# Mixers of the second block: sixteen 256-column fills in three rounded products, with the weight parts made by GpSimd

## The reference, cut to what matters

```python
x = x + 0.5 * swiglu_ffn(x, ffn1_norm[l], ffn1_wi[l], ffn1_wo[l])
h = rms_norm_2(x, mix_norm[l])
(sb_q, sb_k, sb_v, mla_cq, mla_ckv, mla_kr, nsa_q, ck, cv, sk, sv, wk, wv,
 nsa_gate, merge_gate) = jnp.split(h @ w_in[l], offsets, axis=-1)
# three attentions: o_sb, o_mla, o_nsa
y = sigmoid(merge_gate)[0] * (o_sb @ proj_sb[l]) + ...   # three branches
x = x + y @ w_out[l]
x = x + 0.5 * swiglu_ffn(x, ffn2_norm[l], ffn2_wi[l], ffn2_wo[l])
```

## Time and profile before

| | us |
|---|---|
| median of 3 runs (2702.73 to 2706.56) | 2703.87 |
| the profiled execution | 2706.46 |
| its span | 2705.2 |
| first mixer: features begin, attentions begin, output products begin | 1465.7, 1521, 1728.7 |
| second mixer: attentions begin, output products begin | 2235.5, 2444.4 |

### The profile page before, as it was taken

How to read it: one execution, slowest core, us unless ns; L and a number is a source line. 1 busy time by engine, 2 the same in 40 slices (tenths; PEclk the granted TensorE clock), 3 DMA queues, 4 the chain that set the end, 5 groups by cost and what they waited for, 6 DMA issues and landing times.

```text
span 2705.2 us, 28728 instructions
## 1 busy us (share of the span) xinstructions
PE 2298.7 (85%) x12062; PEld 1395.7 (52%) x12062; DVE 1087.7 (40%) x1748; ACT 805.9 (30%) x1178; POOL 1.2 (0%) x5
## 2 busy tenths in 40 slices
PE   7987666667877667666999999999999999999999
PEld 4632111113552111112888644678888885447887
DVE  2331000103651000103765543667667554446774
ACT  3321000002430000002444432544454344235543
POOL 0000000000000000000000000000000000000000
PEclk8999888888989888888999999999999999999999
DMA  9799999999649999999756432356566573225662
GB/s 380 300 369 421 421 422 421 421 422 371 247 156 414 421 421 421 421 421 360 200 189 169 163 108 91 124 146 191 191 174 187 187 197 115 94 78 151 173 191 78
DMA packets 329905, 705.23 MB, mean 261 GB/s; under 512 B 15889, under 2 KB 227089, under 8 KB 277552
## 3 DMA queue, kind: packets, MB, share of 16 engines
q1 hardware_dynamic: 329776, 703.40, 71.0%
HBM read 702.30 MB, written 1.05 MB: 260 GB/s over the span
## 4 chain that ended last, share of the span: by engine, by line
PE 63%; DMA 27%; DVE 5%; ACT 3%; issue 1%; SPq 1%; DVEq 0%; ACTq 0%
PE psum L870 60%; DMA ring<-in_moe_w_up 12%; DMA ring<-in_moe_w_down 6%; DMA ring<-in_moe_w_gate 5%; PE psum L874 3%; DVE arena L2232 1%; DMA arena<-in_moe_w_gate 1%; DMA arena<-in_moe_w_down 1%; DMA arena<-in_moe_w_up 1%; DMA ring<-in_ada_w 1%; ACT ring L1699 1%; DVE lent_r L2232 1%; SPq L712 1%; ACT xn L1699 1%; DVE ring L2232 1%
## 5 line engine op out<-in xcount | busy, mean ns | idle before, releaser
L870 PE MATMUL psum<-ring,arena 128*32 128x512 f32 (+2 forms) x3208 | 607.1, 666 | 243.8 <-DMA ring<-in_moe_w_up 86.0
L870 PE MATMUL psum<-lent_r 128*128 128x512 f32 (+1 forms) x3344 | 610.9, 345 | 3.0 <-DVE lent_r L2232 2.9
L870 PEld LDWEIGHTS psum<-lent_r 128*128 128x128 f32 x3344 | 524.6, 189 | 89.4 <-issue 6.9
L870 PEld LDWEIGHTS psum<-ring,arena 128*32 128x32 f32 (+2 forms) x3208 | 153.5, 128 | 670.1 <-issue 217.4
L2232 DVE TENSOR_TENSOR lent_r<-ring,lent_r 128x2048 fp32r<-128x2048 f32 (+1 forms) x158 | 347.0, 2197 | 206.2 <-ACT lent_r L1699 206.2
L1699 ACT ACTIVATE lent_r<-ring 128x2048 fp32r<-128x2048 f32 (+1 forms) x158 | 290.2, 1842 | 293.0 <-PE psum L870 216.6
L1699 ACT ACTIVATE arena<-psum 128x512 f32<-128x512 f32 (+2 forms) x103 | 55.5, 575 | 826.4 <-PE psum L870 781.3
L870 PE MATMUL psum<-ring,hT 128*128 128x512 f32 x512 | 243.0, 607 | 8.5 <-ACT ring L1699 5.5
L870 PE MATMUL psum<-lent_r,arena_r 128*128 128x512 f32 x1056 | 242.4, 391 | 0.0
L870 PE MATMUL psum<-arena 128*32 128x512 f32 (+6 forms) x648 | 196.4, 497 | 33.4 <-DMA arena<-in_moe_w_up 7.8
L2232 DVE TENSOR_TENSOR arena<-psum,arena 128x512 f32<-128x512 f32 (+2 forms) x21 | 20.3, 978 | 506.1 <-PE psum L870 506.1
(11 more groups left out here) (182 smaller groups left out, 1632.8 us busy)
## 6 DMA issues: line engine op xcount, KB each, us to landing
ring<-in_moe_w_up SPq DMA_DIRECT2D x120, 1024.0 KB, 26.7
ring<-in_moe_w_gate SPq DMA_DIRECT2D x119, 1024.0 KB, 26.7
ring<-in_moe_w_down SPq DMA_DIRECT2D x112, 1024.0 KB, 27.0
ring<-in_ffn_wi SPq DMA_DIRECT2D x176, 512.0 KB, 5.1
ring<-in_w_in SPq DMA_DIRECT2D x46, 1024.0 KB, 5.2
ring<-in_ffn_wo SPq DMA_DIRECT2D x44, 1024.0 KB, 4.9
ring<-in_ada_w SPq DMA_DIRECT2D x43, 1024.0 KB, 10.2
arena<-in_moe_w_gate SPq DMA_DIRECT2D x9, 1024.0 KB, 26.3
```

What stands on the lines that cost most here:

```text
L870: return T.matmul(out, lhsT, rhs, start=start, stop=stop, **kw)
```

## The change

Each mixer's fills become 16 fills of 256 columns (`FILLS`, `FILL_W`) for all 256 tokens: for each of the two token halves 8 x 3 rounded products into one half of bank 7. A fill again has four steps, of twelve products each, and one copy by ScalarE behind it. The rounded high part of a fill's weights is made by GpSimd's `tensor_copy` into one of two slots (`mx.fill_high`), and the low part by GpSimd's `tensor_tensor` in place of the landed weights.

The unsplit `hT` isn't written any more. `mx.hT_high` takes its place in memory, and `mx.hT_low` lies in ring slot 4. Slots 5 and 6 hold the high parts of the weights and slot 7 still NSA's rows. So the ring rotates over slots 0 to 3 in the second block; slots 5 to 7 join it for the loads of a mixer's features and tokens (`order[:0] = extra`) and leave it again behind them (`given_back`).

```diff
 def fill_loads(layer, i):
-    for h in range(2):
-        load(("fill", layer, i, h), E.fill.at(layer, i, 1, h), half_chunk(A["w_in_2"][layer], h, fill_cols[i], 512))
+    for n in (2 * i, 2 * i + 1):
+        load(("fill", layer, n), E.fill.at(layer, n), cols_chunk(A["w_in_2"][layer], fill_cols[n], FILL_W))
...
 def mixer(layer):                                     # SyncE
+    order[:0] = extra
...
+    lend(own[:split_at])
+    given_back.append([owner[n] for n in extra])
...
-        lend(own[:-2])
+        lend(own[:split_at])
...
 def fillers():                                        # TensorE
-    for n in range(8):
-        slots = [got["fill", l, n, s] for s in range(2)]
+    for n in range(FILLS):
+        w = (mx.fill_high[n % 2], rounded_slot(got["fill", l, n][0]))
+        if n:
+            T.wait_ge(*E.filled.at(l, n - 1))
+        T.wait_ge(*E.fill_low.at(l, n))
         for t in range(TT):
-            if n + t:
-                T.wait_ge(*(E.filled.at(l, n, 0) if t else E.filled.at(l, n - 1, 1)))
...
-                    i = mm(psum[:, 7, :], hT[:, s * 4 + k, t * P:(t + 1) * P], slot[:, k * 512:(k + 1) * 512],
-                           s + k == 0, s * 4 + k == KT - 1)
...
+            tok = slice(t * P, (t + 1) * P)
+            for k in range(KT):
+                i = mm3(psum[:, 7, t * FILL_W:(t + 1) * FILL_W], (high[:, k, tok], low[:, k, tok]),
+                        tuple(v[:, k * FILL_W:(k + 1) * FILL_W] for v in w), k == 0, k == KT - 1)
+                if k == 3 or (k == 7 and t == 0):
+                    yield
+        i.then_inc(*E.fill.inc(l, n))
...
-                if k == 0 and u in norm_of_mix:        # VectorE
-                    whole_hT(u, scale, (0,))
...
 def gpsimd_program():
...
+    for layer in range(2):
+        for n in range(FILLS):
+            slot, *landed = got["fill", layer, n]
+            G.wait_ge(*landed)
+            G.wait_ge(*(E.fill.at(layer, n - 2) if n >= 2 else given_back[layer][n]))
+            G.tensor_copy(mx.fill_high[n % 2], slot).then_inc(*pool.own())
+            G.wait_ge(*pool.now)
+            G.tensor_tensor(rounded_slot(slot), slot, mx.fill_high[n % 2].bitcast(F32), ALU.subtract).then_inc(
+                *E.fill_low.inc(layer, n))
```

More of the change, by code:

```diff
@@ L42 @@
 LENT = 6
+SPLIT = 4
+FILLS, FILL_W = 16, 256
 LAST_SLOT = 13024
@@ L317, in build @@
     lent_r = nc.alloc_sbuf_tensor_at("lent_r", [P, LENT * SLOT], F32R, offset=ring_at + (N_SLOT - LENT) * SLOT * 4)
+    hT_r = nc.alloc_sbuf_tensor_at("hT_r", [P, KT, S], F32R, offset=hT_at)
+    own_r = nc.alloc_sbuf_tensor_at("own_r", [P, N_SLOT - LENT, SLOT], F32R, offset=ring_at)
     busy_r = nc.alloc_sbuf_tensor_at("busy_r", [P, 512], F32R, offset=gates_at)
@@ L462, in build @@
     cut_bufs[("mi", 0)] = cut_bufs[("mi", 1)] = [(a.take(SLOT, rounded=True), a.take(SLOT, rounded=True)) for _ in range(2)]
-    mx.hT_high, mx.hT_low = a.take(KT, S, rounded=True), a.take(KT, S, rounded=True)
+    split_at = N_SLOT - LENT - SPLIT
+    mx.hT_high, mx.hT_low = hT_r, own_r[:, split_at, :].rearrange("p (k s) -> p k s", k=KT)
+    mx.fill_high = [own_r[:, split_at + 1 + n, :] for n in range(2)]
     a, r = arena_from(0), lent_from(0)
@@ L608, in build @@
     E.mi_dve = Event(nc, "mi_dve", keys(2, [("f", n) for n in range(0, 10, 2)] + [("t", n) for n in range(2)]))
-    E.fill = Event(nc, "fill", keys(2, 8, TT, 2))
-    E.filled = Event(nc, "filled", keys(2, 8, TT))
+    E.fill_low = Event(nc, "fill_low", keys(2, FILLS))
+    E.fill = Event(nc, "fill", keys(2, FILLS))
+    E.filled = Event(nc, "filled", keys(2, FILLS))
     E.busy = Event(nc, "busy_rows", keys(1))
@@ L641, in build @@
     slot_of = [ring_sb[:, n, :] for n in range(N_SLOT)] + [arena[:, LAST_SLOT:LAST_SLOT + SLOT]]
-    act, dve = Line(nc, "act"), Line(nc, "dve")
-    got = {}
+    act, dve, pool = Line(nc, "act"), Line(nc, "dve"), Line(nc, "pool")
+    got, given_back = {}, []
     E.stored = nc.alloc_semaphore("s_stored")
@@ L663, in parts, with rounded_slot @@
         return cut_bufs[st, c][(p + (st == "ff" and c % 2 == 0)) % 2]
+    def rounded_slot(slot):
+        return own_r[:, next(n for n in range(split_at) if slot_of[n] is slot), :]
     def turned_in(u, k):
@@ L695, in build @@
     at_turns = [8, 9, 10, 11, 0, 1, 2, 3, 4, 5, 6, 7]
-    fill_cols = [C_NQ, C_SK] + [C_MERGE + br * D + n * 512 for br in range(3) for n in range(2)]
+    fill_cols = [c0 + n * FILL_W for c0, width in ((C_NQ, 512), (C_SK, 512), (C_MERGE, 3 * D)) for n in range(width // FILL_W)]
     mi_features = [C_SBQ, C_SBQ + 256, C_SBK, C_SBK + 256, C_CK]
@@ L791, in mixer @@
             w = A["w_in_2"][layer]
+            order[:0] = extra
+            if layer:
+                owner[extra[0]], owner[extra[1]], owner[extra[2]] = E.fill.at(0, FILLS - 2), E.fill.at(0, FILLS - 1), E.ns_pe.at(0, KT - 1)
             for i, c0 in enumerate(mi_features):
@@ L961, in to_hT @@
                     turn(k, 1).then_inc(*E.hT_pe.inc(u, k))
-                T.wait_ge(*(E.hT_whole if u in norm_of_mix else E.hT_dve).at(u, 0))
+                T.wait_ge(*E.hT_dve.at(u, 0))
                 turn(KT - 1, 0)
@@ L1594, in fillers @@
             def fillers():
-                for n in range(8):
-                    slots = [got["fill", l, n, s] for s in range(2)]
-                    for t in range(TT):
-                        if n + t:
-                            T.wait_ge(*(E.filled.at(l, n, 0) if t else E.filled.at(l, n - 1, 1)))
[L1600 to L1603, removed]
-                                i = mm(psum[:, 7, :], hT[:, s * 4 + k, t * P:(t + 1) * P], slot[:, k * 512:(k + 1) * 512],
-                                       s + k == 0, s * 4 + k == KT - 1)
[L1606 to L1611, removed]
+                for n in range(FILLS):
[3 more added lines that the diff above has]
+                    T.wait_ge(*E.fill_low.at(l, n))
+                    for t in range(TT):
+                        tok = slice(t * P, (t + 1) * P)
[5 more added lines that the diff above has]
+                    i.then_inc(*E.fill.inc(l, n))
+                    filled[0] += 1
+                    yield
             def nsa_all():
@@ L1642, in mixer @@
                 if br == 1:
-                    T.wait_ge(*E.filled.at(l, 7, 1))
+                    T.wait_ge(*E.filled.at(l, FILLS - 1))
                 for h in range(2):
@@ L2149, in fillers @@
             def fillers():
[L2150 to L2159, removed]
+                for n in range(FILLS):
+                    yield
+                    yield
+                    yield
+                    C.wait_ge(*E.fill.at(l, n))
+                    out, c0 = ((mx.nq, 0), (mx.kv, 0), (mx.merge[:, 0], 0), (mx.merge[:, 0], 512), (mx.merge[:, 1], 0),
+                               (mx.merge[:, 1], 512), (mx.merge[:, 2], 0), (mx.merge[:, 2], 512))[n // 2]
+                    c0 += n % 2 * FILL_W
+                    af(out[:, :, c0:c0 + FILL_W], psum[:, 7, :].rearrange("p (t c) -> p t c", t=TT), ACT.Copy).then_inc(
+                        *act.ev(E.filled, l, n))
+                    filled[0] += 1
+                    yield
             def nsa_all():
@@ L2171, in nsa_squares @@
                     next(fill)
-                C.wait_ge(*E.filled.at(l, 1, 1))
+                C.wait_ge(*E.filled.at(l, 3))
                 af(xn[:, :, 0:512], mx.nq, ACT.Square)
@@ L2356, in scaled_hT @@
                     *dve.ev(E.hT_dve, u, k))
-                if k == 0 and u in norm_of_mix:
-                    whole_hT(u, scale, (0,))
-        def whole_hT(u, scale, ks):
-            for k in ks:
-                ts(hT[:, k, :], psum[:, turned_in(u, k), 0:S], scale[:, k:k + 1]).then_inc(*dve.ev(E.hT_whole, u, k))
         def add_gated(st, which, u, banks=(0, 1, 2, 3)):
@@ L2888, in over @@
                 return a.unsqueeze(1).unsqueeze(1).broadcast_to([P, 2, 2, n])
+            V.wait_ge(*given_back[l][2])
             for t in range(TT):
@@ L2966, in mixer @@
             scaled_hT(u, mx.hT_high, mx.hT_low, scale)
-            whole_hT(u, scale, (4, 5, 6))
             pieces = cuts("mi", l, 9, False)
```

7 lines of the change are left out of this document (1 added, 6 removed).

## The result

The changed kernel takes 2771.27 us (2768.66 to 2775.01), beside 2704.01 for the kernel before on the same chip: 1.0248 times as long, with an interval of 1.0236 to 1.026. The forecast was 2685 in a range of 2660 to 2715; the change is slower by 67.

The account below looks back on a forecast made before the run. TensorE was taken to bound the mixers, with GpSimd's time free. The terms -39 + 6 + 4 + 10 = -19 gave 2687.5 us for the profiled execution, 2685 as a median; the whole range was 2660 to 2715.

Parts of the forecast that it names:

- The fills: TensorE in both mixers: a fill of 48 products takes 5.82 us, 1.22 less than a unit; 32 give -39.
- Lost cover: Shorter fill steps on TensorE hide less of its waits for VectorE or ScalarE: +3 us a mixer, +6 together.
- GpSimd's pace: GpSimd's copy 1.9, subtraction 3.8 and hand-overs 0.6 make 6.3 us a fill, within the tightest 8.6: cost 0.
- The first fill: At each mixer's start TensorE waits for GpSimd's low part, in the first behind a library reload: +4 us together.
- VectorE beside GpSimd: In the mixers, one in six of GpSimd's 32 pieces costs TensorE a microsecond: +5 us a mixer, +10 together.
- shut out: Rival, chance 0.26: in the mixers GpSimd and VectorE exclude each other in memory; 2724 at 7.5 us a fill.
- The signs named beforehand: Exclusion would show in VectorE's 512-element products well over 0.49 us, or TensorE's VectorE waits over 15 us a mixer.
- What costs nothing: Dropped unsplit rows (-0.2 us a mixer at most), ScalarE's 16 copies, four-slot ring, later loads, VectorE's new wait: no cost.

Follow-up runs that it names:

- quiet: The change with GpSimd's copy and subtraction left out, a constant written instead, loads, waits and products kept: 2671.84 us, 0.9879 of the kernel before.
- memsets: The change with GpSimd writing a constant three times a fill in place of copy and subtraction: 2684.80 us, 0.9922 of the kernel before.

## Why the prediction was wrong, point by point

- *The fills, -39*: right in the mechanism. From 1553.16 to 1554.12 are eight products, 0.12 each, as forecast. Quiet's busy time is 34.4 less, between the forecast's -32 and -39.
- *Lost cover, +6*: 5.8 by quiet's idle time.
- *GpSimd's pace, 6.3 a fill*: it took 1.9 + 4.6 and 0.08 between, 6.6, and TensorE waited for it 0.2 us in the first mixer. Right, but partly by luck: the subtraction was put at 3.8 and the hand-overs at 0.6, and the two errors nearly cancel.
- *The first fill, +4*: the wait for GpSimd itself was 0.15; the reload of the library showed no time at all, the first subtraction starts 0.08 behind the copy, in the second mixer, which has no reload, as in the first. The real cost there was VectorE's, 7.29.

```profile
1517.05 1.90 POOL L3076 CAST own_r<-ring 128x2048 fp32r<-128x2048 f32 x1 [249.35 <-DMA ring<-in_w_in]
1519.03 4.56 POOL L3078 TENSOR_TENSOR own_r<-ring,own_r 128x2048 fp32r<-128x2048 f32 x1
...
1523.63 0.50 PE L887 MATMUL psum<-own_r,hT_r 128*128 128x256 f32 x2 [0.15 <-POOL own_r L3078]
```

- *VectorE beside GpSimd, +10*: **the step that failed.** The change lies 99 us above the run without GpSimd's work. I took one piece in six to cost TensorE a microsecond, with no row that shows how often; a hold lasts up to 4.6 us, it falls on the chains that TensorE reads within a microsecond, and the pauses cost clock on top, a third of the 92.5 us found in the mixers (31.6). That last part wasn't in the term at all.
- *The rival that came true, shut out, 0.26*: the right mechanism with the wrong rule for its price. I asked whether VectorE's and GpSimd's time together fit into the stretch, 94.8 + 16 g. At 6.5 that is 199 of 207, no loss; it is a bound on capacity. What decided is the wait of each result: a fill step has 1.5 us of other work for TensorE, and VectorE was held for up to three times that. Its 2724 was 47 short, and the range's upper end of 2715, taken from the same bound, 56. Nor does every piece exclude every instruction: reductions and reads of PSUM go on.
- *The signs named beforehand* were the right ones: VectorE's products of 512 elements and TensorE's waits for VectorE, 37.8 us in the first mixer where "over 15" was to show it, and 6.34 / 4 = 1.6 us for a product where "well over 0.49" was.
- *What costs nothing*: right. Of the 64.3 us between the two profiled spans (2769.5 - 2705.2), 63.9 lie in the mixers, and quiet has the small ring and the same waits.

## What to carry to other kernels

An idle engine isn't free where it shares a way to the memory with one whose results are awaited: price its work by what one chain that is waited for can meet of it, up to a whole instruction for each of the chain's own, against the spare of the reader. Whether the two engines' times fit into the stretch is only a bound. Here short pieces were the better form of such work (2771 to 2717 by them alone), and the first piece of a stage went to an engine that still had time (2701 to 2693); a place where VectorE has nothing urgent wasn't tried. A pause of TensorE is priced twice, once as waiting and once by the clock behind it (60.9 and 31.6 here).

## What the runs showed of the hardware

GpSimd's subtraction of 2048 elements a row took 4.53 to 5.15 us and its copy 1.89 to 2.36, while three writes took 1.8 each. Sixteen pieces of a copy took 3.85 at the least, twice the whole. VectorE's products of two tensors waited for GpSimd's reads (four took 6.34 in place of 1.97) and not for its writes (0.69 beside one). Its scalings waited for both (3.89 and 1.21 in place of 0.17). Reductions and copies out of PSUM waited for neither: beside a read or a write they kept their 0.42, and of the 34 copies out of PSUM beside GpSimd's reads in the change's mixers and the 44 beside its writes in those of memsets none took over 0.01 us longer than in quiet. Where VectorE and GpSimd wanted the memory at once, they took turns by whole instructions (6.29 and 6.05 for four each).
